# Attention units regrouped: tiles 0 and 1 share a unit, seven units a pair, two output tiles issued at the end of the attention, slope tables made by GpSimd

## The reference

```python
# 8 heads of 64, 2 key/value groups of 4 heads; S = 512 tokens
sc  = qb @ kc - slopes * d_c       # compressed keys (31 of them), masked
p_c = softmax(sc) * (t >= 31)
o_c = p_c @ vc
ss  = qb @ k_sel - slopes * d_s    # selected blocks: 16 of at most 8, so all keys up to t
o_s = softmax(ss) @ v_sel
sw  = qb @ kwb - slopes * d_w      # window of 512 keys, so all keys up to t
o_w = softmax(sw) @ vwb
out = gates[0] * o_c + gates[1] * o_s + gates[2] * o_w
# then
y = concat([rms_norm(rnn), rms_norm(att)]) @ w_out
```

## Time and profile before

| | us |
|---|---|
| median of 3 runs | 1765.19 (1763.97 to 1765.8) |
| the profiled execution's own time | 1764.16 |
| its span in the profile | 1762.3 |
| PE busy in the span | 1735.3 (98%) |
| DVE busy | 1292.5 (73%) |
| ACT busy | 770.2 (44%) |
| POOL busy | 23.2 (1%) |

### The profile page before, as it was taken

One profiled execution on the slowest core, in us unless ns is written; L12 is line 12 of the kernel. 1 busy time (PEld: TensorE's weight loads), 2 busy tenths in 40 slices (PEclk: granted clock), 3 DMA queues, 4 the chain that ended last, 5 costly groups with the idle time before them and its releaser, 6 DMA issues.

```text
span 1762.3 us, 23158 instructions
## 1 busy us (share of the span) xinstructions
PE 1735.3 (98%) x8700; PEld 1406.9 (80%) x8700; DVE 1292.5 (73%) x1890; ACT 770.2 (44%) x1061; POOL 23.2 (1%) x9
## 2 busy tenths in 40 slices
PE   9999999999999999999999999999988999999998
PEld 8896888888888988688888888788755888888886
DVE  6368786886887555877787787866688468777778
ACT  6323442332333513353243243445887365444442
POOL 0000000000000000000000000000100400000000
PEclk9999999999999999999999999999999999999999
DMA  7330434334333233133333333363300222322231
GB/s 275 120 120 25 137 107 142 119 118 142 119 118 119 96 120 110 39 127 130 134 119 124 138 119 119 115 177 120 99 34 2 72 96 96 113 102 96 101 114 49
DMA packets 33210, 194.77 MB, mean 111 GB/s; under 512 B 5744, under 2 KB 7152, under 8 KB 11120
## 3 DMA queue, kind: packets, MB, share of 16 engines
q1 hardware_dynamic: 24656, 156.77, 25.8%
q10 hardware_dynamic: 8480, 36.97, 6.5%
HBM read 186.91 MB, written 2.11 MB: 107 GB/s over the span
## 4 chain that ended last, share of the span: by engine, by line
PE 89%; DVE 5%; issue 3%; ACT 2%; DMA 1%; SPq 0%; DVEq 0%; ACTq 0%; PEldq 0%
PE ps L558 28%; PE ps L560 28%; PE ps L559 28%; PE ps L708 1%; PE ps L722 1%; DVE pb L2384 1%; DMA raw<-in_weights 1%; DVE acc L2593 1%; DMA both<-in_weights 1%; PE ps L730 0%; PE ps L980 0%; PE ps L895 0%; DVE wl L1865 0%; DMA x<-in_xin 0%; DVE acc L2603 0%
## 5 line engine op out<-in xcount | busy, mean ns | idle before, releaser
L558 PE MATMUL ps<-xh,wh 128*128 128x512 f32 x1440 | 566.8, 394 | 5.4 <-DVE xl L1824 2.5
L560 PE MATMUL ps<-xh,wl 128*128 128x512 f32 x1440 | 561.0, 390 | 0.0
L559 PE MATMUL ps<-xl,wh 128*128 128x512 f32 x1440 | 560.4, 389 | 0.0
L1149 ACT ACTIVATE wh<-raw 128x2048 fp32r<-128x2048 f32 x128 | 244.6, 1912 | 284.1 <-DMA raw<-in_weights 280.6
L558 PEld LDWEIGHTS ps<-xh,wh 128*128 128x128 f32 x1440 | 270.4, 188 | 65.8 <-issue 9.0
L560 PEld LDWEIGHTS ps<-xh,wl 128*128 128x128 f32 x1440 | 270.3, 188 | 57.0
L559 PEld LDWEIGHTS ps<-xl,wh 128*128 128x128 f32 x1440 | 270.5, 188 | 56.2 <-issue 1.4
L1865 DVE TENSOR_TENSOR wl<-raw,wh 128x2048 fp32r<-128x2048 f32 x108 | 246.7, 2285 | 91.4 <-ACT wh L1149 91.4
L1376 ACT ACTIVATE cv<-upb,prm 128x512 f32<-128x512 f32 x88 | 67.0, 809 | 251.5 <-DVE upb L2065 251.5
L558 PE MATMUL ps<-wh,xh 128*128 128x256 f32 (+1 forms) x352 | 107.9, 307 | 0.0
L560 PE MATMUL ps<-wh,xl 128*128 128x256 f32 (+1 forms) x352 | 106.4, 302 | 0.0
(11 more groups left out here) (326 smaller groups left out, 2577.4 us busy)
## 6 DMA issues: line engine op xcount, KB each, us to landing
raw<-in_weights SPq DMA_DIRECT2D x129, 1024.0 KB, 4.8
adab<-in_ada ACTq DMA_DIRECT2D x22, 1024.0 KB, 4.8
both<-in_weights SPq DMA_DIRECT2D x7, 2048.0 KB, 7.5
t<-in_cst ACTq DMA_DIRECT2D x1, 3200.0 KB, 10.2
x<-in_xin SPq DMA_DIRECT2D x8, 256.0 KB, 6.1
turned<-q ACTq DMA_DIRECT2D x8, 256.0 KB, 4.1
turned<-k ACTq DMA_DIRECT2D x8, 256.0 KB, 4.6
adab_tail<-in_ada ACTq DMA_DIRECT2D x2, 1024.0 KB, 11.8
```

What stands on the lines that cost most here:

```text
L558: pe.matmul(out, w_hi, m_hi, start=start, stop=False)
L559: pe.matmul(out, w_hi, m_lo, start=False, stop=False)
L560: return pe.matmul(out, w_lo, m_hi, start=False, stop=stop)
L1149: act.activation(wh[:, s, :], raw[:, s, :], ACT.Copy).then_inc(hi_made, 1)
```

## The change

The units of a pair are listed in a table. Tiles 0 and 1 of a branch now form one unit whose two pieces lie side by side in the bank (128 and 256 columns, 384 together). There are seven units a pair and 28 in all, in the order: branch 0 tile 2, tile 3, tiles 0 and 1; branch 1 tiles 0 and 1, tile 3, tile 2; compressed. Each step loops over the pieces of a unit and signals once per head. DVE does `weigh` of the compressed unit ahead of the next pair's first `minima`. The slope tables of pairs 1 to 3 are made by GpSimd between the low halves of `WO2` and `WO2 + 1`, and no longer by ACT. `out_tokens` of `WO2` for tile 2 stands before the last `turn`, for tile 3 before the last `values`; tiles 0 and 1 follow, and the ones product after them.

```diff
-HIGH_AT = (3, 6, 7, 8)
-RNN_SCALED_AT = (9, 11, 13)
-RNN_HIGH_AT = (12, 14, 16, 17)
-RNN_LOW_AT = (14, 16, 18, 19)
+UNIT_TILES = ((0, (2,)), (0, (3,)), (0, (0, 1)), (1, (0, 1)), (1, (3,)), (1, (2,)), None)
+PER = len(UNIT_TILES)
+SIGNALS = 2 * PER - 1
+HIGH_AT = (2, 4, 5, 6)
+RNN_SCALED_AT = (PER, PER + 2, PER + 4)
+RNN_HIGH_AT = (PER + 3, PER + 5, 2 * PER - 1, 2 * PER)
+RNN_LOW_AT = (PER + 5, 2 * PER - 1, 2 * PER, 2 * PER + 1)
...
+        def pieces(tiles):
+
+            at = 0
+            for i in tiles:
+                yield i, at, (i + 1) * P
+                at += (i + 1) * P
...
             low(OWN, OWN % RING)
+            pool.wait_ge(staged2, 2)
+            for r in range(1, 4):
+                if r >= 2:
+                    pool.wait_ge(sc_done, unit_signals(PER * (r - 1) - 1))
+                for g in range(2):
+                    pool.tensor_scalar(tsl[:, r % 2, g, :], alibi, slopes[:, r + 4 * g:r + 4 * g + 1], None, ALU.mult).then_inc(staged2, 1)
             pool.wait_ge(sq_added, SQ_RNN + 6)
...
+                if U == UNITS - 1:
+                    pe.wait_ge(rnn_low, 4)
+                    pe.wait_ge(*split(WO2))
+                    pe.wait_ge(sc_done, unit_signals(UNITS - 2))
+                    out_tokens(WO2, 0, 2, (0, 1, 2, 3), True, False)
                 turn(U)
                 if U:
                     values(U - 1)
+            out_tokens(WO2, 0, 3, (0, 1, 2, 3), True, False)
             values(UNITS - 1)
...
-            pe.wait_ge(rnn_low, 4)
-            pe.wait_ge(*split(WO2))
-            for i in range(NT):
-                if i == 2:
-                    pe.wait_ge(att_evac, 4)
-                    pe.wait_ge(sq_added, SQ_RNN + 6)
-                    pe.matmul(bank(7), ones, std[:, :], start=True, stop=True).then_inc(sq4_used, 1)
+            pe.wait_ge(sc_done, unit_signals(UNITS - 1))
+            for i in range(2):
                 last = out_tokens(WO2, 0, i, (0, 1, 2, 3), True, False)
             last.then_inc(slab_used, 1)
+            pe.wait_ge(att_evac, 4)
+            pe.wait_ge(sq_added, SQ_RNN + 6)
+            pe.matmul(bank(7), ones, std[:, :], start=True, stop=True).then_inc(sq4_used, 1)
...
-                if v in (4, 5) and r < 3:
-                    stage(r + 1, (v - 4,))
...
-                if v < 8:
-                    w = (v % 4 + 1) * P
+                if tiles:
                     for g in range(2):
-                        at = 2 * v + g
-                        dve.memset(soft[:, 3, at:at + 1], 0.0)
-                        dve.tensor_tensor_reduce(out=pb[:, U % 3, g, 0:w], in0=ps[:, 2 * ((U + 1) % 2) + g, 0:w], in1=tsl[:, r % 2, g, S - w:S],
-                                                 scale=1.0, scalar=3e38, op0=ALU.add, op1=ALU.min,
-                                                 accum_out=soft[:, 0, at:at + 1]).then_inc(sc_done, 1)
+                        for i, at, w in pieces(tiles):
+                            c = 8 * b + 2 * i + g
+                            dve.memset(soft[:, 3, c:c + 1], 0.0)
+                            ins = dve.tensor_tensor_reduce(out=pb[:, U % 3, g, at:at + w], in0=ps[:, 2 * ((U + 1) % 2) + g, at:at + w],
+                                                           in1=tsl[:, r % 2, g, S - w:S], scale=1.0, scalar=3e38, op0=ALU.add, op1=ALU.min,
+                                                           accum_out=soft[:, 0, c:c + 1])
+                        ins.then_inc(sc_done, 1)
...
             for U in range(UNITS):
+                if U % PER == PER - 1:
+                    weigh(U)
                 if U + 1 < UNITS:
                     minima(U + 1)
-                weigh(U)
+                if U % PER < PER - 1:
+                    weigh(U)
```

More of the change, by code:

```diff
@@ L474, in unit_signals, with unit, unit_width @@
         def unit_signals(U):
-            return U // 9 * 17 + min(2 * (U % 9 + 1), 17)
+            return U // PER * SIGNALS + min(2 * (U % PER + 1), SIGNALS)
+        def unit(U):
+            r, v = divmod(U, PER)
+            b, tiles = UNIT_TILES[v] or (None, None)
+            return r, b, tiles
+        def pieces(tiles):
[3 more added lines that the diff above has]
+                at += (i + 1) * P
+        def unit_width(tiles):
+            return sum(i + 1 for i in tiles) * P
         @block.sync
@@ L976, in turn @@
                 for g in range(2):
[L977 to L979 removed]
+                    pe.wait_ge(p_ready, unit_signals(U) - (1 - g if tiles else 0))
+                    if tiles:
+                        for j in range(unit_width(tiles) // P):
                             last = pe.transpose(ps[:, 4 + g, j * P:(j + 1) * P], pb[:, U % 3, g, j * P:(j + 1) * P], ident)
@@ L986, in values, with out_tokens @@
             def values(U):
-                r, v = divmod(U, 9)
+                r, b, tiles = unit(U)
                 pe.wait_ge(pt_evac, U + 1)
-                if v == 0 and r >= 2:
+                if U % PER == 0 and r >= 2:
                     pe.wait_ge(att_evac, r - 1)
-                i, b = v % 4, v // 4
-                for j in range(i + 1) if v < 8 else (0,):
-                    for g, h in enumerate(halves):
[L995 to L1000, removed]
-                last.then_inc(values_used, 1)
+                if tiles:
+                    for i, at, w in pieces(tiles):
+                        for j in range(i + 1):
+                            for g, h in enumerate(halves):
+                                last = pe.matmul(ps[h, 6 + r % 2, i * P:(i + 1) * P], vv[:, j, b * P + HD * g:b * P + HD * g + HD],
+                                                 pt[:, U % 2, g, at // P + j, :], start=(U % PER == 0 and j == 0), stop=False)
+                else:
+                    for g, h in enumerate(halves):
+                        last = pe.matmul(ps[h, 6 + r % 2, :], vcs[0:N_CMP, HD * g:HD * g + HD], ptc[0:N_CMP, g, :],
+                                         start=False, stop=True)
+                last.then_inc(values_used, 1)
+            def out_tokens(n, f, i, kts, start, stop):
+                s = n % RING
+                for c, kt in enumerate(kts):
+                    w = slice((kt % 4) * S, (kt % 4 + 1) * S)
+                    last = product(bank(NT * f + i), xh[:, kt, tokens(i)], xl[:, kt, tokens(i)], wh[:, s, w], wl[:, s, w],
+                                   start and c == 0, stop and c == len(kts) - 1)
+                return last
             pe.wait_ge(proj2_evac, 6)
@@ L1572, in keep_turned @@
             def keep_turned(U):
-                v = U % 9
+                tiles = unit(U)[2]
                 act.wait_ge(t_done, U + 1)
```

83 lines of the change are left out of this document (41 added, 42 removed).

## The result

The changed kernel takes 1754.73 us (median of 5 runs, 1754.50 to 1755.44) where the kernel before takes 1763.99 us (5 runs on the same chips, 1763.90 to 1765.80). The ratio is 0.9945, 95% interval 0.9931 to 0.9959, so it is faster by about 9.7 us by the ratio, 9.3 between the two medians. The forecast was 1758.7, a gain of 6.5, in a range from 1755.3 to 1763.2: right in sign, too small by a third, and just outside the range.

The account below looks back on a forecast made before the run. PE's 10.04 us of idle time in the attention was taken as the bound. Gain 10.04 - 3.1 - 0.4 - 0.5 = 6.0, plus 0.5, 6.5 us: median 1758.7 us, range 1755.3 to 1763.2.

Parts of the forecast that it names:

- Part 1: PE's work in the attention: matmuls same in number and shape, only regrouped, so costed at zero; busy time 83.08 us.
- PE's real work 82 rather than 83.08: Attention: the view counts drains as busy, so PE's idle time is nearer 11 us; half taken, 0.5 us more gain.
- Part 2: Attention regrouping: PE's cover exceeds DVE's need in every unit by at least 0.16 us; 3.1 us of idle time stay.
- The start: First units of the attention, now larger: PE idles 1.1 us before the first turn, then 0.3; 1.4 us taken.
- The last unit: End of the attention: output tiles 2 and 3, 2.72 us, fully cover PE's waits for ACT's copies, at no cost.
- Part 3: Behind the attention: PE newly waits 0.4 us for GpSimd's low half of slab `WO2 + 1`.
- Part 4: Slope tables on GpSimd, 1.15 us an operation, disturb DVE; some 0.5 us reaches PE, bounds 0 and 18.4.
- Rival C: Attention near the full bound: start filled better, no disturbance; gain 9 us, time 1756.2, chance 0.14.
- Rival D: Last minima of pairs 0 and 1: GpSimd's table operations stop DVE, slower at 1775.0 us, chance 0.05.
- Rival B: Behind the attention GpSimd's slab work binds, PE waits 2.4 us; gain 4.5, time 1760.7, chance 0.10.
- Rival A: Attention handovers, with little slack at units 3 and 5, swallow half the gain; gain 2.5, time 1762.7, chance 0.14.
- rival E: Attention stalls move from `turn` to waits on ACT's copies `pt`; gain 0, time 1765 us, chance 0.06.

Follow-up runs that it names:

- merge_only: Kernel before with only tiles 0 and 1 merged into one unit, old tile order, tables on ACT, old end and old compressed `weigh` order: 1755.84 us.
- split_units: Changed kernel with tiles 0 and 1 in units of their own again, nine units a pair, in the new order: 1763.56 us.
- runs_cut_all: Changed kernel with PE's turn and values runs cut in two in 24 rounds, same matmuls: 1760.59 us.
- runs_cut_some: Changed kernel with PE's turn and values runs cut in two in only 8 rounds, where both merged units turn: 1756.83 us.
- end_undone: Changed kernel with output tiles 2 and 3 behind the attention again, the ones product between the second and third tile: 1753.73 us.
- tables_on_act: Changed kernel with the slope tables made by ACT again, none on GpSimd: 1753.16 us.
- better: Changed kernel with output tile 2 before the turn of unit 26 and scores 1 before the compressed keys on PE: 1752.80 us.

## Why the prediction missed

**The failing step is Part 1, "I cost this at zero".** It took PE's work as fixed because number and shape of matmuls don't change. From it follows the bound that opens the prediction, that the change can win no more than PE's 10.04 us of idle time, and so the low end of the range. But PE's busy time in the stage fell by 3.76 us: the merge took away 24 runs (three for each of eight merged units) at a fixed part of 0.155 to 0.21 each, 4.2 us (3.9 by the distances in pair 1), and the output tiles between attention runs put 0.34 back. `merge_only` gives 4.26 for the first, `split_units` 4.12, `runs_cut_all` and `runs_cut_some` 0.28 and 0.26 for two runs. The numbers lay in the earlier trace rows: turns of 4, 6 and 8 blocks cost 0.58, 0.78 and 1.00, which goes to 0.16 and not to zero for no blocks. In the covers I took the merged turn as one run (0.78) but added values and scores of tiles 0 and 1 as two runs, 0.96 and 1.05; they cost 0.81 and 0.85. And the sum took no gain from fewer runs anywhere.

With the measured 3.8 in this place, the sum would have been 6.0 + 3.8 = 9.8 against the stage's 9.49. The 0.5 us that I added for "PE's real work 82 rather than 83.08" is another thing. The 82 is added up from the old, smaller runs, so their fixed parts are in it. (Its 6.6 for the turns should be 6.5; the 20.0 is right.) The prediction's own reason fits the rows: before a gap the busy time holds the whole last instruction, 0.07 us more than the distance that counts in a row (1.13 against 1.06 for scores of 512 columns). With 13 marked gaps before and 6 after, that is up to 0.5 us of the 3.76, an estimate; no run separates it.

The other steps:
- Part 2, need and cover: right for the changed kernel. The regular stalls went, the compressed unit and the unit of 512 columns no longer stall a steady pair. In `merge_only` one shortfall came out at 0.28 where the rule gave 0.3. In `split_units` it missed half of the added idle time, and in `merge_only` one gap by 0.6. The rule looks at one unit and doesn't carry over what DVE is behind from the one before; that this is the reason is not shown.
- The start: 1.4 forecast, 1.99 measured. Unit 26: 0.7 forecast, 0.84. Pair 1's extras and other handovers: 0.5 each forecast, 0.26 in all beyond the marked gaps.
- The last unit: that the tiles cover the waits is right, but the waits were 0.70 us and not worth the move (`end_undone`).
- Part 3: 0.4 forecast, 0.22 measured; GpSimd started 2.18 us behind the last values, as forecast.
- Part 4: 0.5 forecast, 0.70 by `tables_on_act`. GpSimd's operation takes 1.56 to 1.75 us, not 1.15 by length from L540. DVE rows got longer beside GpSimd's, which the prediction named as a sign of being wrong, and its price was about right.
- Idle time in all: 4.0 forecast (3.1 + 0.4 + 0.5), 4.31 measured. That this comes so near is in part luck: the start was 0.6 above its term, other stalls below theirs.
- The forecast stood on the median of 1765.19. With more runs the kernel before is at 1763.99, and the same gain of 6.5 from there would have given 1757.5. That is the smaller part of the miss.

Rival C (gain 9, "start filled better, no disturbance") came nearest in size but not in cause. Rival D is excluded: GpSimd's operation delays DVE by 0.4 us. Rival B's wait was 0.22 us. Rival A's stalls at units 3 and 5 are there only where GpSimd works (0.40 and 0.60 at unit 5), and rival E's waits for ACT's copies are not marked at all.

## What to carry to other kernels

When small matmuls or transposes of different kinds take turns on PE, read the cost of a run against its length and take the value at length zero: it is paid once a run, and merging or regrouping runs wins it even where PE shows no idle time at all. For a pipeline over three engines, write down for each unit what the slow engine must do between two events and what PE has to do meanwhile; equal-sized units win most here. The order brings less: by the stages 1.4 us without the merge (`split_units` against before) and 2.0 with it (`tables_on_act` against `merge_only`), each with small other parts in it. Idle time is not the bound of what a regrouping can win.

## What was not expected of the hardware

- The fixed part of a PE run: 0.16 us for transposes of 128 x 128 fp32, 0.155 for value products (128 x 64 weights), 0.21 for scores with two heads side by side. Whether it is the change of array shape, of the kind of instruction or the drain of the last one, these runs don't tell apart; it was paid at each change between these three kinds. One place hints that the array shape has a part in it. In `better` a turn of six blocks (128*128 in the row) follows an output tile, also 128*128, and takes 0.75 us from start to start, where it takes 0.81 behind `scores` (64*128):

```profile
1354.86 0.82 PE L1008 MATMUL ps<-keep,pb 128*128 128x128 f32 x6
1355.61 1.09 PE L1024 MATMUL ps<-pt,vv 128*64 128x128 f32 x16
```

- GpSimd multiplies a 128 x 512 fp32 table by a column in 1.56 to 1.75 us (six of them, 9.7 us), 3.0 to 3.4 ns a column, where its subtraction L540 takes 2.24 ns a column of 2048. The 1.75 are the two that start together with a DVE scaling.
- A DVE `tensor_scalar` that starts with a GpSimd operation takes 0.40 us more, while GpSimd works for 1.75 us. The Trainium skill, page "SBUF — State Buffer", section "Who interferes with whom", has a DVE operation in a two-port mode and a GpSimd operation exclude each other, the later fully blocked for the whole of the first. The measurement differs: no DVE operation lost more than 0.41 us to a GpSimd operation. Of those with both inputs in SBUF one lost 0.39 us (L2427 at 1295.80), and two lost nothing beside it (0.68 and 0.42 us, at 1315.00 and 1316.54). GpSimd's spans in a profile are rough, so part of its 1.75 us may not be use of the port.
